# Eight filling products between the router's logits and the count of ranks

## The reference, cut to what matters

```python
lg = (xf @ w_rg).astype(jnp.float32) + b_rg.astype(jnp.float32)
grp = jnp.argmax(lg, axis=-1)
...
le = jnp.take_along_axis(le, grp[:, None, None], axis=1)[:, 0]
top_v, top_i = lax.top_k(le, TOP_K)
gate = p_grp * jax.nn.softmax(top_v, axis=-1)
expert = grp[:, None].astype(jnp.int32) * EXPERTS_PER_GROUP + top_i.astype(jnp.int32)
...
order = jnp.argsort(e_flat)
...
return (jax.nn.silu(xb @ w_gate[e]) * (xb @ w_up[e])) @ w_down[e]
```

## Time and profile before

| | |
|---|---|
| median of three runs | 1574.41 us (1572.16 to 1574.76) |
| the profiled execution's own time | 1573.33 us |
| its span | 1571.5 us |
| TensorE matmul busy | 1357.7 us, 86% |
| TensorE weight load busy | 759.8 us, 48% |
| VectorE busy | 395.9 us, 25% |
| ScalarE busy | 315.9 us, 20% |
| GpSimd busy | 190.5 us, 12% |
| mean DMA rate over the span | 301 GB/s |
| mean granted TensorE clock | 0.96 |

### The profile page before, as it was taken

One profiled execution on the slowest core, in us unless ns is written; L12 is line 12 of the kernel. 1 busy time (PEld: TensorE's weight loads), 2 busy tenths in 40 slices (PEclk: granted clock), 3 DMA queues, 4 the chain that ended last, 5 costly groups with the idle time before them and its releaser, 6 DMA issues. The chain is left out here.

```text
span 1571.5 us, 17845 instructions
## 1 busy us (share of the span) xinstructions
PE 1357.7 (86%) x6818; PEld 759.8 (48%) x6818; DVE 395.9 (25%) x747; ACT 315.9 (20%) x609; POOL 190.5 (12%) x309
## 2 busy tenths in 40 slices
PE   5999996999878788877999988997998887888886
PEld 4999774333322222223789765783333322222232
DVE  3344524000000000003635678524000000000003
ACT  5212221111010101012533357430110001010002
POOL 2000001111111111111000000001111111111111
PEclk9999997999999999999999989998999999999999
DMA  9130447999999999997423210466999999999995
GB/s 341 61 108 1 161 161 295 408 426 425 423 426 427 426 424 423 427 425 295 138 78 105 80 55 1 161 245 247 417 425 424 426 426 425 424 423 425 418 426 205
DMA packets 63099, 473.75 MB, mean 301 GB/s; under 512 B 11232, under 2 KB 11308, under 8 KB 38976
## 3 DMA queue, kind: packets, MB, share of 16 engines
q1 hardware_dynamic: 48656, 442.55, 68.5%
q0 software_dynamic: 14384, 30.36, 5.2%
HBM read 465.17 MB, written 23.13 MB: 311 GB/s over the span
## 5 line engine op out<-in xcount | busy, mean ns | idle before, releaser
L1148 PE MATMUL ps<-ring,act 128*64 128x512 f32 x1792 | 445.2, 650 | 75.6 <-DMA ring<-in_e_up 63.6
L1148 PEld LDWEIGHTS ps<-ring,act 128*64 128x64 f32 x1792 | 141.5, 143 | 374.2 <-issue 374.2
L1706 DVE TENSOR_TENSOR act<-act,ps 128x256 f32<-128x256 f32 x64 | 27.0, 422 | 867.9 <-ACT act L918 867.9
L1171 PE MATMUL ps<-ring,act 128*64 128x512 f32 x896 | 204.6, 597 | 31.0 <-ACT act L920 31.0
L1074 PE MATMUL ps<-parts 128*128 128x264 f32 x1152 | 143.8, 287 | 4.5 <-DVE parts L1497 2.9
L1074 PEld LDWEIGHTS ps<-parts 128*128 128x128 f32 x1152 | 142.5, 190 | 5.5 <-issue 5.5
L1101 PE MATMUL ps<-parts 128*128 128x512 f32 x552 | 132.8, 398 | 4.2 <-DVE parts L1505 3.2
L918 ACT ACTIVATE act<-ps 128x256 f32<-128x256 f32 x64 | 24.6, 384 | 552.2 <-PE ps L1148 552.2
L1171 PEld LDWEIGHTS ps<-ring,act 128*64 128x64 f32 x896 | 70.8, 136 | 126.2 <-issue 126.2
L1101 PEld LDWEIGHTS ps<-parts 128*128 128x128 f32 x552 | 103.1, 189 | 30.2 <-issue 4.0
L1373 PE MATMUL ps<-parts 128*128 128x264 f32 (+1 forms) x576 | 92.4, 322 | 1.2 <-PE ps L1373 0.9
(11 more groups left out here) (217 smaller groups left out, 1082.8 us busy)
## 6 DMA issues: line engine op xcount, KB each, us to landing
ring<-in_e_gate SPq DMA_DIRECT2D x56, 2048.0 KB, 17.7
ring<-in_e_up SPq DMA_DIRECT2D x56, 2048.0 KB, 22.2
ring<-in_e_down SPq DMA_DIRECT2D x56, 2048.0 KB, 22.2
arena<-in_e_down SPq DMA_DIRECT2D x8, 2048.0 KB, 16.2
ring<-in_a_w_in SPq DMA_DIRECT2D x6, 2048.0 KB, 19.7
arena<-in_e_up SPq DMA_DIRECT2D x6, 2048.0 KB, 19.7
arena<-in_e_gate SPq DMA_DIRECT2D x6, 2048.0 KB, 14.5
ring<-in_w_kv SPq DMA_DIRECT2D x4, 2048.0 KB, 13.2
```

Source lines behind the costliest of these rows:

```text
L1148: last = mm(ps[f * C:(f + 1) * C, 2 + b, :].rearrange("p (g m i) -> p g m i", g=2, i=2), x, w, start=(k == 0), stop=(k == KC - 1))
L1171: last = mm(ps[o * C:(o + 1) * C, 6 + b, :], hT[:, b, (2 * c + a) * C:(2 * c + a + 1) * C], w[:, f * D + o * DH:f * D + (o + 1) * DH], sta ...
```

## The change

After the opening product of `count_rows`, and before the wait for the membership table, TensorE issues eight more products into bank 7, of the shape and operands of the three at L1229. Nothing reads them. This happens once in each layer. No wait and no semaphore is added, and no other engine's program changes.

```diff
 WARM = 3
+WARM_RANKS = 8
...
                 mm(ranks, ones, bcast(upper[:, 0], (nt + 1) * E, 1), start=True, stop=False)
+                for n in range(WARM_RANKS):
+                    mm(ps[:, 7, :], ident, h[:, 0, 0:W], start=True, stop=True)
                 pe.wait_ge(members, 2 * layer + 2)
```

## The result

The kernel with the eight products takes 1580.26 us (median of eight runs, 1577.69 to 1583.57) against 1574.59 us (1569.23 to 1576.16) before. The ratio is 1.0041, with a 95% interval of 1.0028 to 1.0054: slower by 6.5 us, between 4.4 and 8.5 (the two medians alone differ by 5.7). The prediction said 1578.7 us in a range of 1575 to 1583, and slower; both held. Beside the later experiments the same kernel ran twelve times more and came out at 1.0029 (1.0018 to 1.0041), 4.6 us. Four executions of the experiments ran at a lower granted clock (0.65 to 0.84) and took 1627 to 1960 us; the ratios leave them out, and where one of them was the profiled one, that of the version with the first layer only, another profile stands in its place.

A forecast was written before the change was run, and what follows sets the result against it. Weight transfers, restarted by the first expert, were taken to bound the kernel. Later starts of 3.1 us plus 1.2 for half clock there gave 4.3 us, on the median 1574.41 a forecast of 1578.7 us, range 1575 to 1583.

The forecast's parts named there:

- What bounds the kernel: Expert stages: weight transfers set the pace, so moving the first expert's start moves the end by as much.
- The price of the eight: Behind each layer's opening count product: eight take 8.9 us, making the next count product 2.3 and 2.8 us late.
- c = 4: Time the eight products spend at half clock in each layer, taken as 4 us, within bounds of 2 and 6.
- The credits: Faster count products save 0.7 and 0.5 us by layer; turns no longer held by L1229 save 0.8, first layer only.
- The sum of this part: First expert's start in both layers: 0.8 us late in the first, 2.3 in the second, together 3.1 us.
- The first expert at half clock: TensorE idles longer ahead of the first expert and may lose the clock: 1.2 us for both layers, bounds 0 and 3.4.
- The clock that stays up: During the eight, c is near 0: 1573.5 us, not slower; chance 0.12, including a clock that nearly stays up.
- The clock that stays down: Clock doesn't return during the eight: they take 13.7 us, kernel 13.9 us slower, 1588.3 us; chance 0.05.
- The lost gain: Clock falls ahead of the first expert in both layers: 6.5 us slower, 1580.9 us, or 1582.9 with c = 6; chance 0.12.
- the third term: The clock at the start of the first expert: 1.2 us lost over both layers, bounds 0 and 3.4.
- The order of the matmuls: On TensorE count products cannot pass the eight; if they could, the sum would be the credits alone, -2.0 us.

The follow-up runs named there:

- sixteen: Sixteen filling products instead of eight at the same place, against the kernel with the eight: 1591.52 us, ratio to before 1.0113.
- four and five: Against the kernel with eight: four ahead of the membership table, two ahead of the slot tables, five instead of three behind them; 1571.84 us, 0.9994 of before.
- eight and six: Against the kernel with the eight: six instead of three filling products behind the slot tables; 1579.49 us, ratio to before 1.0037.
- eight and five: Against the kernel with the eight: five instead of three filling products behind the slot tables; 1580.67 us, ratio to before 1.0037.

## Why the prediction was right, point by point

**What bounds the kernel.** Right. The start of the first expert, and more precisely the first transfer that its products release, moved by 5.2 us, the third to the thirtieth by 6.6, and the time by 4.6 to 6.5.

**The price of the eight.** Right within 10%. Predicted 8.9 us with c = 4; the clock came back after 3.4 and 3.8 us, and the next count product followed the first of the eight after 8.20 and 8.40 us. Measured from the opening product it came 1.6 us late in the first layer (8.38 against 6.80; predicted 2.3) and 2.3 in the second (8.68 against 6.37; predicted 2.8). The row of that product starts before the last filling record ends (253.36 against 245.16 + 8.76 = 253.92), so the ranks are the better measure: late by 1.1 us (254.82 - 244.98 against 251.31 - 242.59; predicted 1.6) and 2.1 (1073.67 - 1063.86 against 1068.67 - 1060.94; predicted 2.3). The second layer's gather followed, 2.1 us late (1079.97 - 1063.86 against 1074.97 - 1060.94; predicted 2.3).

**The credits.** Right in kind, some too large. The faster count products were to give 0.7 and 0.5 us; from their first start to the ranks 0.5 and 0.2 were made up. Behind the first step, which takes 0.46 us (253.36 to 253.82), they stand 0.13 us apart, as predicted. The 0.8 us of the turns that L1229 held (the prediction has it at half clock to 260.6; the clock was back at about 260.1) is 1.1 - 0.3: in the first layer the ranks were 1.1 us late and the first expert 0.3. In the second layer the 2.1 us arrived as 2.0. The sum of this part was predicted as 3.1 us and measured as 2.3.

**The first expert at half clock.** That the clock would be lost there was right (why it is lost is argued, see what stays open); the size wasn't, and this is the term that was most wrong. The prediction took 1.2 us for both layers together, within bounds of 0 and 3.4: 0.7 of one loss of 1.7, the price of 3.4 us at half clock. By the first transfer, which followed the first expert's start by 3.71 us (270.52 - 266.81) and 3.35 (1087.92 - 1084.57) against 2.05 in both layers before, it measured 1.7 + 1.3 = 3.0 us. By the third and the later ones it measured the whole lengthening of the products, 10.16 - 7.42 = 2.7 and 9.03 - 7.42 = 1.6, together 4.3 us, which is above the upper bound. The price was right for the second layer, where the half clock lasted 3.4 us (1085.0 to 1088.4) and cost 1.6. In the first it lasted 5.8 us of the expert's products (266.8 to 272.6), and that both layers would be hit was not expected. So 4.3 us was predicted and 2.3 + 4.3 = 6.6 found in the transfers, with the first part too large by 0.8 and this one too small by 3.1. That the two errors have opposite signs is luck, and it brought the sum nearer.

**The rivals.** The clock that stays up needed c below 0.9 us; it was 3.4 and 3.8. The clock that stays down needed no rise during the eight; there was one in both layers. The lost gain, with half clock at both first experts, is what the third term turned out to be in the profiles; at c = 4 that rival gave 6.5 us and it was put at a chance of 0.12; six of six profiled layers with the eight and three behind had it, so that was too low.

**The order of the matmuls.** The Trainium skill, in "TensorE: Matmul & The Clock Gate" (Part 2), has matmuls keep the program's order. The traces with eight and with sixteen agree: the count products need only the table, and with the table long written they still did not start ahead of the last filling product, at 253.36 behind eight (table at 251.73) and at 263.01 behind sixteen (table at 253.76).

**What stays open.** Four points. That the clock is lost at the first expert because TensorE idles more ahead of it is argued and not shown: it was kept in all four profiled layers of the versions with four and five, and with eight and six, but in neither layer of the one with eight and five. The versions that fill the gap behind the slot tables too made the transfers of their profiles earlier, and not the time beyond its interval; half clock during their own filling explains one layer of one profile, not the rest. How much of the late transfers reaches the end can't be read from single profiles. From the first layer's opening product to the last instruction it is 1328.9 and 1324.4 us in the two profiles of before, 1333.3 and 1331.6 in the two with eight, and 1343.1 with sixteen: 5.8 and 16.4 us more on average, where the third transfers are 6.6 and 19.2 late, but the same kernel differs by 4.5 from one execution to the next. And a part of the scatter of the times (some 7 us between the fastest and the slowest run of before in the first series) lies ahead of the first layer's opening product, which starts at 242.6 to 247.2 us in the profiles of these kernels, though the code ahead of it is the same.

## What to carry to other kernels

Filling products to keep the clock up delay what is behind them as soon as they end later than the data that the next real product waits for. Count them at the clock that they will find, not at the one that they are to bring: here eight products took 8.2 to 8.4 us in gaps of 6.8 and 6.4, of which 3.4 to 3.8 at half clock, while four of them, or eight of 32 columns, cost nothing that could be measured. What a higher clock can give back is bounded by the work that runs next and is waited for, here under 1 us of count products and 0.8 of held turns; look that up before the filling is sized. Then follow the clock to the next dense stage, and price half clock there by all the products whose buffers are waited for and not by the first: here this was the larger part, 4.3 of 6.6 us.

## What the runs showed that was not expected

The clock fell to half just as dense products began (at about 245.3 us, with the eight from 245.16 on), after TensorE had run the small logits products and turns, busy 1.00, 0.97 and 0.65 of the three microseconds from 242 to 245. In the second layer of the kernel before it fell in a microsecond in which TensorE was busy throughout. So a busy row is no sign that the clock will be there for the next products; here they ran at half for 3.4 us. And unchanged code may keep the full clock through its first expert in one execution (264.14 us, 7.42 us long) and lose it 0.7 us into it in another (268.22, 8.94 us long), so that one profile of a short stage is not enough to price a change of 0.1%.
